# The recurrence of a gated linear-attention mixer: the order of its steps on each engine

## What is computed

```
def step(S, inp):
    r_t, w_t, kk_t, b_t, v_t, k_t = inp
    sa = jnp.einsum("bhvk,bhk->bhv", S, kk_t)
    S = (S * w_t[:, :, None, :] - sa[..., None] * b_t[:, :, None, :]
         + v_t[..., None] * k_t[:, :, None, :])
    return S, jnp.einsum("bhvk,bhk->bhv", S, r_t)
```

## Time and profile before

| | us |
|---|---|
| median of 3 runs | 1566.12 (1564.27 to 1566.78) |
| the profiled execution | 1564.46 |
| its span, first to last instruction | 1562.8 |
| TensorE busy (matmul) | 1473.9, 94% |
| TensorE weight loads | 1221.7, 78% |
| VectorE busy | 912.4, 58% |
| ScalarE busy | 598.7, 38% |
| GpSimd busy | 268.9, 17% |
| mean granted clock of TensorE | 0.98 |
| products at L884 (the solve and updates) | 152.8 in 4224 records |

### The profile page before, as it was taken

The page is one execution under the profiler, slowest core; times in us unless marked ns, Lnnn a source line. Parts: engine busy times, 40 slices in busy tenths (PEclk is TensorE's granted clock), DMA queues, the critical chain, the costliest instruction groups (busy, mean ns, idle before and its releaser), DMA issues.

```text
span 1562.8 us, 35515 instructions
## 1 busy us (share of the span) xinstructions
PE 1473.9 (94%) x14858; PEld 1221.7 (78%) x14858; DVE 912.4 (58%) x1499; ACT 598.7 (38%) x1037; POOL 268.9 (17%) x290
## 2 busy tenths in 40 slices
PE   6999988999998989999999998999989999999997
PEld 3788866888888767788777886877878888888885
DVE  4424245777677648888885224766565655655232
ACT  4422344444343434434343224535664223322221
POOL 0100023554452010111110211000021111111110
PEclk9999998999999899999999999999999999999999
DMA  9232201332300231323222331312103233232221
GB/s 372 98 109 81 80 2 57 104 98 86 110 4 4 82 108 54 107 81 107 81 99 93 102 106 59 114 56 68 67 30 103 88 105 102 86 107 93 93 92 72
DMA packets 38986, 139.14 MB, mean 89 GB/s; under 512 B 3152, under 2 KB 3664, under 8 KB 38480
## 3 DMA queue, kind: packets, MB, share of 16 engines
q1 hardware_dynamic: 38720, 135.24, 25.6%
q10 hardware_dynamic: 144, 2.10, 0.4%
HBM read 135.22 MB, written 2.10 MB: 88 GB/s over the span
## 4 chain that ended last, share of the span: by engine, by line
PE 77%; DVE 15%; ACT 3%; issue 3%; DMA 1%; DVEq 0%; ACTq 0%; SPq 0%
PE bank L702 56%; PE bank L884 7%; DVE ffn_sb L2935 5%; PE bank L711 3%; PE bank L648 2%; DVE arena L2654 1%; DVE w_up L2436 1%; PE bank L1019 1%; DMA arena<-w 1%; PE bank L641 1%; PE bank L974 1%; ACT w_up L1571 1%; PE bank L985 1%; ACT arena L2026 1%; DVE w_in L2436 1%
## 5 line engine op out<-in xcount | busy, mean ns | idle before, releaser
L702 PE MATMUL bank<-hf_hi,w_up 128*128 128x512 f32 x1376 | 424.1, 389 | 0.0
L702 PEld LDWEIGHTS bank<-hf_hi,w_up 128*128 128x128 f32 x1376 | 258.3, 188 | 53.2
L702 PE MATMUL bank<-hf_lo,w_up 128*128 128x512 f32 x688 | 269.2, 391 | 4.5 <-DVE w_up L2436 4.5
L702 PE MATMUL bank<-act_hi,w_down 128*128 128x512 f32 x704 | 216.7, 389 | 0.0
L1571 ACT ACTIVATE w_up<-ring 128x1024 fp32r<-128x1024 f32 x87 | 91.9, 1058 | 215.7 <-PE bank L702 215.7
L884 PE MATMUL bank<-arena 64*64 64x32 f32 (+1 forms) x4224 | 152.8, 226 | 15.1 <-DVE arena L2611 9.2
L884 PEld LDWEIGHTS bank<-arena 64*64 64x64 f32 x4224 | 142.6, 142 | 29.7 <-issue 11.3
L2436 DVE TENSOR_TENSOR w_up<-ring,w_up 128x1024 fp32r<-128x1024 f32 x87 | 106.9, 1229 | 97.0 <-ACT w_up L1571 97.0
L702 PEld LDWEIGHTS bank<-hf_lo,w_up 128*128 128x128 f32 x688 | 129.1, 188 | 36.2 <-DVE w_up L2436 9.1
L2935 DVE SCALAR_TENSOR_TENSOR ffn_sb<-ffn_sb 128x512 f32<-128x512 f32 x176 | 151.5, 861 | 5.4
L702 PEld LDWEIGHTS bank<-act_hi,w_down 128*128 128x128 f32 x704 | 132.2, 188 | 27.4
(11 more groups left out here) (351 smaller groups left out, 2343.9 us busy)
## 6 DMA issues: line engine op xcount, KB each, us to landing
ring<-w SPq DMA_DIRECT2D x76, 1024.0 KB, 4.9
ring<-w SPq DMA_DIRECT2D x32, 704.0 KB, 4.0
ring<-w SPq DMA_DIRECT2D x64, 256.0 KB, 3.0
arena<-w SPq DMA_DIRECT2D x8, 1024.0 KB, 19.1
x<-xT SPq DMA_DIRECT2D x1, 2048.0 KB, 9.5
...
arena<-ctxT SPq DMA_DIRECT2D x1, 1024.0 KB, 19.6
```

What stands on the lines that cost most here:

```text
L702: ins = mm(out, w[:, a, k, :], of_block(b, k0 + k), start=first and k == 0 and m == 0, stop=last and k == n - 1 and m == 2)
```

## The change

The steps are written out operation by operation for each engine, in two loops: one for n = 0 and 1 (context) and one for n = 2 to 10, with the first solve (n = -1) ahead of them and a tail behind. No product, copy or transfer is added or left out. The core of it:

- In n = 2 to 10, `scores` of chunk q stand at level 2 (direction 1 ahead of dx 2, direction 0 behind it), and VectorE takes them at levels 2 and 3. In n = 0 and 1 they stay at level 5.
- `state_in` of chunk m is mixed, half a direction at a time, into the products nx 4 and dx 4 of the same chunk's solve. Only chunk 0 has its own.
- `updates` and `state_terms` stay at levels 2 and 3, `results` stand between dx 3 and nx 4 and between nx 4 and dx 4, `turned` at level 5 (in the token steps), the modulation rows at level 6, one slot between dx 5 and nx 6 and one between nx 6 and dx 6; their selection follows a step later.
- The token gates' products stand in pairs between every two level products of the first solve.
- VectorE's, ScalarE's and SyncE's orders follow. ScalarE makes the exponentials one chunk earlier, GpSimd the keys.
- A third buffer of scores lies in free gates, the keys of even token chunks in a free part of kT, and `plast` has four places for three.
- Early returns (`if q >= NC: return` and the like) in the helpers keep the set of operations.

```diff
@@ buffers and SyncE
+def keys_at(d, q):
+
+  if q < NCC or q % 2:
+    return scans[d].bk
+  return kT[:, :, 2 * L * d:2 * L * d + 2 * L].rearrange("p j (e t) -> p j e t", e=2)
+
+def scores_at(d, q):
+
+  if q < NCC:
+    return scans[d].nk[:, q % 2]
+  return scans[d].nk[:, (q + 2) % 3] if (q + 2) % 3 < 2 else nk_third[d]
...
+  def pace(m, u, e):
+
+    if m < NCC - 1:
+      return m, 2 * (3 + 2 * u) + e
+    return m + 1, 2 * 2 + 3 * u + e
+
   def load_paced(g, at, m, u):
 
     sp.wait_ge(s["product"], DONE[g - 2])
     to = ring[:, g % 2, :].rearrange("p (c n) -> p c n", c=2)
     for e in range(PARTS):
-      l = 3 + 2 * u + e // 2
-      sp.wait_ge(s[("nx_mm0", "dx_mm0")[e % 2]], 5 * m + l - 1)
+      step, l = pace(m, u, e)
+      sp.wait_ge(s[("nx_mm0", "dx_mm0")[l % 2]], 5 * step + l // 2 - 1)
@@ TensorE: helpers
+  def state_begun(n, d, j):
+
+    sc, out = scans[d], bank[d][3][:, L * j:L * j + L]
+    for r in HALVES:
+      mm(out[across(r)], sc.ktrt[r, n % 3, j, 0:L], sc.S[r, n % 2, j, :], start=True, stop=False)
+
+  def state_ended(n, d, j):
+
+    nk, v_in, out = scores_at(d, n), values(d, n), bank[d][3][:, L * j:L * j + L]
+    for e, r in enumerate(HALVES):
+      last = mm(out[across(r)], nk[r, e, j, 0:L], v_in[r, e, j, :], start=False, stop=True)
+    if j == NJ - 1:
+      last.then_inc(s[f"gu_mm{d}"], 1)
...
+  def state_quarter(n, d, first):
+
+    def part(j):
+      block = first + j // 2
+      if j % 2 == 0:
+        state_begun(n, d, block)
+      else:
+        state_ended(n, d, block)
+
+    return part
...
+    if l == 4 and m > 0:
+      state_ready(m, d)
+    tiles(lambda j, r: bank[d][2][r, 32 * j:32 * j + 32], lambda j, r: nk[r, 1 - head(r), j, 0:L],
+       lambda j, r: side(sc.X[r, j, :], l, d),
+       beside=state_quarter(m, d, 0) if l == 4 and m > 0 else None).then_inc(s[f"nx_mm{d}"], 1)
...
@@ TensorE: the context steps
+  for n in range(NCC - 2):
+    m, q = n + 1, n + 2
+    if n == 0:
+      state_in(n, 1)
+    ada_part(n, 0)
+    turned(m, 0)
+    if n == 0:
+      state_in(n, 0)
+    nx(m, 1, 2)
+    nx(m, 0, 2)
+    updates(n, 1)
+    dx(m, 1, 2)
+    updates(n, 0)
+    dx(m, 0, 2)
+    turned(m, 1)
+    nx(m, 1, 3)
+    state_terms(n, 0)
+    state_terms(n, 1)
+    dx(m, 1, 3)
+    nx(m, 0, 3)
+    dx(m, 0, 3)
+    nx(m, 1, 4)
+    ada_part(n, 1)
+    nx(m, 0, 4)
+    dx(m, 1, 4)
+    dx(m, 0, 4)
+    nx(m, 1, 5)
+    nx(m, 0, 5)
+    scores(q, 0)
+    dx(m, 0, 5)
+    ada_select(n)
+    nx(m, 0, 6)
+    dx(m, 1, 5)
+    scores(q, 1)
+    nx(m, 1, 6)
+    dx(m, 0, 6)
+    dx(m, 1, 6)
@@ TensorE: the token steps
+  for n in range(NCC - 2, NC - 1):
+    m, q = n + 1, n + 2
+    nx(m, 0, 2)
+    nx(m, 1, 2)
+    scores(q, 1)
+    updates(n, 0)
+    dx(m, 1, 2)
+    dx(m, 0, 2)
+    scores(q, 0)
+    updates(n, 1)
+    nx(m, 1, 3)
+    nx(m, 0, 3)
+    state_terms(n, 0)
+    if n == NC - 2:
+      gate_products(0, 1)
+    state_terms(n, 1)
+    if n == NC - 2:
+      gate_products(1, 2)
+    if n > NCC - 2:
+      ada_select(n - 1)
+    dx(m, 1, 3)
+    dx(m, 0, 3)
+    results(n, 0)
+    nx(m, 0, 4)
+    nx(m, 1, 4)
+    results(n, 1)
+    dx(m, 0, 4)
+    dx(m, 1, 4)
+    nx(m, 0, 5)
+    turned(m, 0)
+    nx(m, 1, 5)
+    dx(m, 0, 5)
+    turned(m, 1)
+    dx(m, 1, 5)
+    ada_part(n, 0)
+    nx(m, 0, 6)
+    nx(m, 1, 6)
+    ada_part(n, 1)
+    dx(m, 0, 6)
+    dx(m, 1, 6)
+  for d in both:
+    updates(NC - 1, d)
+  for d in both:
+    done("Y", d, 5 * NC)
+  gate_products(2, NJ)
+  for d in both:
+    results(NC - 1, d)
@@ ScalarE: the token steps
+  for n in range(NCC - 2, NC - 1):
+    m, q = n + 1, n + 2
+    keys_in(q + 1)
+    update_out(n, 0)
+    update_out(n, 1)
+    if n == NC - 2:
+      for d in range(2):
+        done("kh", d, 2 * NC)
+        done("rt", d, NCX)
+      for j in range(4):
+        act_f(ycv[0][:, j, :], y_conv[:, j, :], ACT.Copy).then_inc(s["h_hi"], 1)
+    decay_exps(q + 1)
+    update_in(m, 1)
+    first_result(n, 0)
+    first_result(n, 1)
+    tok_out(m, 0)
+    state_padded(m, 0)
+    tok_out(m, 1)
+    state_padded(m, 1)
+    update_in(m, 0)
+    ada_row_out(n)
+  split_first("W_OUT")
+  for d in range(2):
+    update_out(NC - 1, d)
@@ VectorE: the context steps from w 5 on
+  for n in range(-1, NCC - 2):
...
+    w_out(m, 0, 5)
+    scores_out(q, 0)
+    x_out(m, 0, 5)
+    mod_out(n)
+    w_out(m, 1, 5)
+    first_level(q, 0)
+    x_out(m, 1, 5)
+    x_turned(m, 1, 5)
+    w_out(m, 0, 6)
+    w_out(m, 1, 6)
+    x_turned(m, 0, 5)
+    scores_out(q, 1)
+    first_level(q, 1)
+    first_turned(q, 1)
+    y_last(m, 1)
+    y_last(m, 0)
+    first_turned(q, 0)
@@ VectorE: the token steps
+  for n in range(NCC - 2, NC - 1):
+    m, q = n + 1, n + 2
+    running_sums(q + 1, 0)
+    w_out(m, 1, 2)
+    w_out(m, 0, 2)
+    scores_out(q, 1)
+    x_out(m, 1, 2)
+    x_out(m, 0, 2)
+    x_turned(m, 0, 2)
+    scores_out(q, 0)
+    x_turned(m, 1, 2)
+    w_out(m, 1, 3)
+    w_out(m, 0, 3)
+    state_out(n, 0)
+    if n > NCC - 2:
+      mod_out(n - 1)
+    state_out(n, 1)
+    x_out(m, 0, 3)
+    x_out(m, 1, 3)
+    running_sums(q + 1, 1)
+    x_turned(m, 0, 3)
+    if n == NC - 2:
+      conv_low(0)
+    w_out(m, 0, 4)
+    w_out(m, 1, 4)
+    second_result(n, 0)
+    x_turned(m, 1, 3)
+    if n == NC - 2:
+      conv_low(1)
+    x_out(m, 0, 4)
+    x_turned(m, 0, 4)
+    if n == NC - 2:
+      conv_low(2)
+    x_out(m, 1, 4)
+    x_turned(m, 1, 4)
+    if n == NC - 2:
+      conv_low(3)
+    w_out(m, 0, 5)
+    first_level(q, 1)
+    w_out(m, 1, 5)
+    first_level(q, 0)
+    x_out(m, 0, 5)
+    x_turned(m, 0, 5)
+    x_out(m, 1, 5)
+    w_out(m, 0, 6)
+    x_turned(m, 1, 5)
+    w_out(m, 1, 6)
+    first_turned(q, 0)
+    first_turned(q, 1)
+    y_last(m, 0)
+    second_result(n, 1)
+    y_last(m, 1)
@@ GpSimd: its loop over chunks
-      done("tok_mm", d, q)
+      done("tok_mm", d, q if q < NCC else q - 1)
```

482 lines of the change are left out of this document (243 added, 239 removed).

## The result

The changed kernel takes 1580.65 us (median of 4 runs, 1578.33 to 1585.86), the kernel before 1565.19 on the same chip: ratio 1.0111, 95% interval 1.0093 to 1.0129. It is slower by 15 to 17 us where the forecast was 12 faster. The profiled execution took 1581.83 (span 1580.2, mean granted clock 0.961; before 1562.8 and 0.980).

A forecast was written before the change was run, and what follows sets the result against it. TensorE in the first block's recurrence was taken as the bound, losing 27.5 us to VectorE waits and clock falls; 16.0 stays, 0.5 comes from gates, gain 12.0, forecast 1554.1 us, range 1546 to 1563.

The forecast's parts named there:

- Clock: Recurrence, twelve steps: fewer pauses should mean fewer falls of the clock; three falls left, 3.3 us, bounds none and six.
- slower, by the clock: Rival, chance 0.06: turned keys beside pauses and pausing context steps make 18 clock falls in place of 6; 1570.6 us.
- Mixing of the state products: State products within level 4: 1.87 us a step either way, mixing priced at nothing; bounds 3 more, 2 less.
- VectorE at the end of a step: Old step end: VectorE takes scores and finishes levels 5 and 6 while TensorE sits 1.13 us for a w row.
- the walk: Hand-timed token step, TensorE at 0: n=3 to 6 lose 0.3 us each, n=7 to 9 lose 0.9 or more.
- First solve: Gates in pairs over all levels, modulation rows split: spacing a little more even, gain 0.5 us, bounds -1.5 to +2.
- Context steps: Steps n=0 and 1: TensorE waits 1.8 us a step; with 1.9 in n=2, 5.5 lost for n=0 to 2.
- Weight pieces at nothing: From the third chunk on, pieces go out at levels 2 to 5 of the step using them; cost nothing.
- Turned keys at level 5: Moved from level 3 to between nx(0,5) and nx(1,5), beside pauses; a possible cause of clock falls.
- Last step and tail: Loss of 1.2 us for 3.3 in n=10, and of 0.9 for 2.4 in the tail.
- GpSimd's circle: Turned keys, GpSimd's keys, next scores(1): 21.0 us, 21.3 with selection; uncovered at n=7 and 8, each losing 1.5.
- The ceiling: Recurrence: idle time of weight loads, 37.9 us, as most that could be gained; the prediction kept 27.5.

The follow-up runs named there:

- e2: Changed kernel with the state products in one piece instead of mixed into level 4: 1573.6 us, ratio 1.0078.
- e14: e13 with the state products of the token steps mixed into level 4 again: 1572.9 us, ratio 1.0043.
- e13: e11 with the turned keys of n=0 back behind nx of level 3: 1566.8 us, ratio 1.0029.
- e10: e9 with the state products of the token steps mixed into level 4 again: 1580.0 us, ratio 1.0100.
- e9: Changed kernel with first solve and context steps in the old order on TensorE, VectorE and ScalarE, state products in one piece: 1580.4 us, ratio 1.0106.
- e11: e9 with context steps' turned keys moved ahead of nx of level 2 and ScalarE's chunk-2 exponentials behind its first update copies: 1567.9 us, ratio 1.0028.
- e1: Changed kernel with the first solve's gate pairs and modulation rows back in the old order: 1584.5 us, ratio 1.0142.
- e4: Changed kernel with the weight pieces released as before, at levels 3 to 6 of the step ahead: 1583.6 us, ratio 1.0141.
- e3: Changed kernel with the turned keys of the token steps back at level 3: 1597.3 us, ratio 1.0226.

## Why the prediction was wrong

**The step that failed is "Clock"**: "twelve steps with fewer pauses should fall less often: I take three falls, 3.3 us". The half clock doubled, 37.6 to 78.5 us. At 0.4 us lost for each (step 3 against step 2: 27.8 - 19.3 - 1.7 of pause = 6.8 for 17 us), 41 us more cost about 16, more than the 11.7 lost between the marks; and the fetch pauses, for which the prediction had no term at all, took 5.2 us more than before. The rival "slower, by the clock", 1570.6 with a chance of 0.06, is what came, by more than its price. But not by its mechanism: it asked for 18 falls in place of 6, and there were seven from step 0 on. They were longer: it took falls as pieces of 1.1 us, the price of 3.4 us at half clock, though the last of the six in the kernel before was already 10.2 us long; one fall here was 17 us long and cost 6.8. The sign was open, and three falls should not have stood beside a bound of six as if the change could only help. What sets the length of a fall stays open.

**Mixing of the state products**, "I price the mixing at nothing", bounds -3 to +2. The rate was wrong: the mixed products run in about half the time, 0.9 us less for each of two products a step. Little of that reaches the step (step 2 takes 19.3 for 19.4 in e2), and the clock falls more. By medians mixing cost 4.5 us (e2) and 6 (e14 against e13), neither beyond doubt, and nothing (e10 against e9); the lower clock is clear of noise in the first two.

**VectorE at the end of a step.** Right in the main: the w-row waits of 8.5 us in the eight token steps went to 1.9. Not foreseen were 4.5 us at x rows; in e13 all waits for VectorE in these steps are 1.7. Without its falls the walk's gain for the eight steps is 6.0 us (13.0 of waits before, 7.0 after). Unmixed, they took 172.3 us in e11, 173.6 in e2, 174.5 in e9 and 176.6 in e13, against 176.9 before: 0.3 to 4.6 less, and where the half clock in them is as before (13.7 us), 4.6 in e11 and 2.4 in e9. So the token order is a gain, of less than the walk said.

**First solve**, "a gain of 0.5; bounds -1.5 to +2": it lost 5.2. TensorE's waits there for VectorE and ScalarE, changed kernel, then before:

```profile
PEld bank L904 <- DVE arena L2768: 4.0, 4, 1.5
PEld bank L904 <- DVE arena L2816: 2.8, 1, 2.8
PEld bank L904 <- DVE arena L2777: 2.3, 2, 1.5
```

```profile
PEld bank L884 <- DVE arena L2648: 2.8, 1, 2.8
PEld bank L884 <- ACT arena L1767: 0.7, 1, 0.7
```

New are 6.3 us for w and x rows, and 10.2 us more at half clock. With the gates in the old order on TensorE (e1) the half clock went and the time stayed; with the old order on all three engines (e9) TensorE stood 3.9 us for ScalarE's exponentials; with those moved too (e13) the stretch is where it was, 41.4. e11's 40.4 has 3.4 us less half clock and is no gain of the order.

**Context steps**, "5.5 for n=0 to 2" lost: they took 24.0 and 23.9, before 22.3 and 20.6. The forecast had them at 18.7 plus about 2. At full clock I have no stretch to compare, 10.2 and 6.8 us of them being half clock. TensorE waits 4.8 us for VectorE and 1.1 for GpSimd in them, before 0.8; how much of the loss is order and how much clock is not separated by any run.

**Weight pieces at nothing**: right as far as time can tell; in e4's trace the old places have more time in fetch pauses. **Turned keys at level 5**: the new place is the better one (e3), so the turned keys' new place, which the prediction weighed as a risk for the clock, is not what slowed this kernel. **Last step and tail**: forecast gain 3.6; 1.0 came, in e11 and e13 2.4 and 3.2, and 1.05 of each is work that moved ahead of the mark. **GpSimd's circle**: seen where it was forecast, at n=8. Scores(1) stood 1.13 us and began 0.2 behind the last key product (TensorE, then GpSimd):

```profile
464.74 0.21 PEld L999 LDWEIGHTS bank<-arena 64*64 64x64 f32 x2 [1.13 <-issue]
```

```profile
459.45 5.11 POOL L2372 TENSOR_TENSOR arena<-arena,rstd 64x256 f32<-64x256 f32 x6 [0.65 <-PE bank L1011]
```

That step 8 took 21.0, as forecast, is luck, since 3.4 us of it are at half clock. Step 9 (19.1) can't be set against the forecast of 20.3: between the marks it holds no scores, 1.8 us. **The ceiling** by weight loads, 37.9, was never near: nothing was gained to compare it with. **Outside** the recurrence the time was to stay within 1 us; it moved by 5.7, with 19 us more at half clock, in code that is the same.

What no run explains: e3's clock of 0.79; why e11 and e13 scatter over 18 and 22 us when the kernel before stays within 8 beside them (in both the slow runs have the low clock); what sets a fall off and how it chooses its length. No kernel here beats the one before outside its uncertainty.
